# Another order for TensorE in two attention stages: transposes inside the query projection, the second query ahead of the first scores, two output tiles interleaved

## The reference, cut to what matters

```
q = (rmsnorm(q_lat) @ w_uq).reshape(B, S, 8, 128 + 64)      # nope and rope parts
kv = (rmsnorm(kv_lat) @ w_ukv).reshape(B, S, 8, 128 + 128)  # k_nope and v
s = (q_nope k_nope^T + rope(q_rope) rope(k_rope)^T) * scale, causal
y_mla = softmax(s) v * silu(g_mla)
mix = concat([y_mla, y_pool, y_conv]); out = mix @ w_out + b_out
x = layernorm(ALPHA * x + out)
```

```
logits = q k^T * scale + (F[t] - F[s]), causal;  F = cumsum(log_sigmoid(f))
y_b = softmax(logits) v * silu(g_b)
x = x + gate * (concat([y_a, y_b]) @ w_out);  out = rms_norm(x)
```

## Time and profile before

| | us |
|---|---|
| median of 3 runs | 2412.99 (2410.28 to 2414.29) |
| the profiled execution, its time | 2410.3 |
| its span, first to last instruction | 2408.3 |
| TensorE busy | 2355.2 (98%) |
| VectorE busy | 1262.3 (52%) |
| ScalarE busy | 875.1 (36%) |
| GpSimd busy | 411.3 (17%) |
| mean granted clock of TensorE | 0.993 |

### The profile page before, as it was taken

The page is one execution under the profiler, slowest core; times in us unless marked ns, Lnnn a source line. Parts: engine busy times, 40 slices in busy tenths (PEclk is TensorE's granted clock), DMA queues, the critical chain, the costliest instruction groups (busy, mean ns, idle before and its releaser), DMA issues.

```text
span 2408.3 us, 31276 instructions
## 1 busy us (share of the span) xinstructions
PE 2355.2 (98%) x11360; PEld 1954.6 (81%) x11360; DVE 1262.3 (52%) x1970; ACT 875.1 (36%) x1332; POOL 411.3 (17%) x402
## 2 busy tenths in 40 slices
PE   7999999999999999999999999999999999999998
PEld 5888888888887888888788887788878888887887
DVE  8555543476556456543466777643254444444334
ACT  5422223365225422222365223422234444444221
POOL 4111100033113211100042112212002222222000
PEclk9999999999999999999999999999999999999999
DMA  6555553212322555553212323423322222223332
GB/s 245 186 190 177 175 182 113 70 62 70 102 90 71 197 174 174 178 170 131 87 53 71 96 88 112 157 88 105 96 79 88 78 78 78 78 74 133 101 102 79
DMA packets 80906, 281.90 MB, mean 117 GB/s; under 512 B 8896, under 2 KB 13248, under 8 KB 79936
## 3 DMA queue, kind: packets, MB, share of 16 engines
q1 hardware_dynamic: 63968, 217.49, 27.6%
q0 software_dynamic: 16864, 63.45, 7.7%
HBM read 272.51 MB, written 8.39 MB: 117 GB/s over the span
## 4 chain that ended last, share of the span: by engine, by line
PE 81%; issue 8%; DVE 5%; ACT 3%; POOL 1%; DMA 1%; SPq 0%; ACTq 0%; DVEq 0%
PE bank L341 25%; PE bank L343 25%; PE bank L342 25%; DVE w_lo L335 1%; PE bank L2144 1%; ACT w_hi L312 1%; DMA w_raw<-stream 1%; DVE q_rope L1435 0%; DVE bank L1552 0%; DVE x_res L1130 0%; PE bank L2224 0%; PE bank L2225 0%; DVE x_lo L1222 0%; DVE mix_lo L1558 0%; PE bank L2067 0%
## 5 line engine op out<-in xcount | busy, mean ns | idle before, releaser
L343 PE MATMUL bank<-x_hi,w_hi 128*128 128x512 f32 x2896 | 1126.2, 389 | 0.0
L342 PE MATMUL bank<-x_hi,w_lo 128*128 128x512 f32 x2896 | 1125.8, 389 | 0.0
L341 PE MATMUL bank<-x_lo,w_hi 128*128 128x512 f32 (+1 forms) x2384 | 941.8, 395 | 8.3 <-POOL x_lo L418 3.7
L335 DVE SCALAR_TENSOR_TENSOR w_lo<-w_raw,w_hi 128x1024 fp32r<-128x1024 f32 (+1 forms) x384 | 475.5, 1242 | 733.7 <-ACT w_hi L312 732.6
L312 ACT ACTIVATE w_hi<-w_raw 128x1024 fp32r<-128x1024 f32 x390 | 407.7, 1048 | 942.6 <-PE bank L343 903.0
L343 PEld LDWEIGHTS bank<-x_hi,w_hi 128*128 128x128 f32 x2896 | 544.0, 188 | 113.5
L342 PEld LDWEIGHTS bank<-x_hi,w_lo 128*128 128x128 f32 x2896 | 544.9, 188 | 107.1 <-issue 2.2
L341 PEld LDWEIGHTS bank<-x_lo,w_hi 128*128 128x128 f32 x2384 | 448.2, 188 | 101.1 <-issue 6.1
L341 PE MATMUL bank<-mix_lo,w_hi 128*128 128x512 f32 (+1 forms) x656 | 255.3, 389 | 1.1 <-issue 0.9
L425 POOL TENSOR_SCALAR probs<-probs,stats 128x128 f32<-128x128 f32 (+3 forms) x128 | 138.4, 1087 | 643.8 <-DVE stats L1541 643.8
L341 PEld LDWEIGHTS bank<-mix_lo,w_hi 128*128 128x128 f32 x656 | 123.9, 189 | 26.2 <-issue 1.4
(11 more groups left out here) (337 smaller groups left out, 2158.7 us busy)
## 6 DMA issues: line engine op xcount, KB each, us to landing
w_raw<-stream SPq DMA_DIRECT2D x390, 512.0 KB, 3.5
ada_w<-wada POOLq DMA_DIRECT2D x96, 512.0 KB, 4.8
x_tokens<-xN SPq DMA_DIRECT2D x4, 1024.0 KB, 8.7
x_res<-xT SPq DMA_DIRECT2D x16, 256.0 KB, 10.6
x_res_spill<-x_res POOLq DMA_DIRECT2D x8, 512.0 KB, 6.1
x_res<-x_res_spill POOLq DMA_DIRECT2D x8, 512.0 KB, 7.5
outT<-x_res SPq DMA_DIRECT2D x16, 256.0 KB, 2.2
cond_b<-cond POOLq DMA_DIRECT2D x2, 1024.0 KB, 6.1
```

What stands on the lines that cost most here:

```text
L335: nc.vector.scalar_tensor_tensor(out=WL[:, slot, :cols[n]], in0=RAW[:, slot, :cols[n]], scalar=1.0, in1=WH[:, slot, :cols[n]].bitcast(F32) ...
L341: nc.tensor.matmul(out, wh, xl, start=first, stop=False)
L342: nc.tensor.matmul(out, wl, xh, start=False, stop=False)
L343: return nc.tensor.matmul(out, wh, xh, start=False, stop=last)
```

## The change

It alters only the order of instructions: TensorE's in three places, and one ScalarE instruction.

- Heads 2 to 7: `trans1` of blocks 0 and 1 moves from ahead of the query projection to the middle of it, behind its second step.
- Heads 0 and 1: `q_proj(1)` moves ahead of the scores of head 0. In head 1 the value projection comes ahead of block 2's transposes and of the rope projection.
- The first two output tiles of a layer are issued as one list of 32 steps: steps 0 to 14 of the first, 0 to 9 of the second, step 15 of the first, 10 to 15 of the second. The transposes of head 7 come one block at a time behind steps 1, 3, 6 and 9, `pv1` behind steps 7 and 12.
- Second block, first pair: its scores lie at steps 7, 10, 13 and 15.
- Second block, last pair: the work at steps 7, 9, 11, 13 goes to 10, 12, 15, 17, and ScalarE does the last gate right behind the last exponential.

```diff
@@ scalar
             softmax_exp(last, 3, BANKS_2)
+            gate(PAIRS - 1)
             for i in range(QB):
                 for k in MIX_BEHIND[i]:
                     mix2(k)
                 pt_hi(last, i)
-                if i == 1:
-                    gate(PAIRS - 1)
@@ tensor, project(out, u, cols, k0, kt, mid={})
                                         XH[:, k0 + k, :], XL[:, k0 + k, :], k == 0, k == kt - 1)
+                        for work in mid.get(k, ()):
+                            work()
@@ tensor, layer
+                def tr(h, *blocks):
+                    return lambda: [trans1(h, i) for i in blocks]
                 for h in range(HEADS):
                     k_proj(h)
-                    if h:
-                        trans1(h - 1, 0)
-                        trans1(h - 1, 1)
-                    q_proj(h)
-                    if h:
-                        trans1(h - 1, 2)
-                    if h % 2 and h < HEADS - 1:
-                        rope_proj(h // 2 + 1)
-                    v_proj(h)
+                    if h == 0:
+                        q_proj(0)
+                        v_proj(0)
+                        q_proj(1)
+                    elif h == 1:
+                        tr(0, 0, 1)()
+                        v_proj(1)
+                        tr(0, 2)()
+                        rope_proj(1)
+                    else:
+                        q_proj(h, {1: [tr(h - 1, 0, 1)]})
+                        tr(h - 1, 2)()
+                        if h % 2 and h < HEADS - 1:
+                            rope_proj(h // 2 + 1)
+                        v_proj(h)
...
-                tile(l, T_OUT, 0, (S["mix_lo"], KT * l), MIX_ORDER, source=mix,
-                     mid={0: [tr(0), tr(1)], 3: [tr(2)], 4: [pr(0)], 6: [tr(3)], 9: [pr(1)]})
-                tile(l, T_OUT + 1, 1, order=MIX_ORDER, source=mix)
+                def out_pair(mid):
+                    steps = [(0, n) for n in range(KT - 1)] + [(1, n) for n in range(10)]
+                    steps += [(0, KT - 1)] + [(1, n) for n in range(10, KT)]
+                    for at_step, (t, n) in enumerate(steps):
...
+                        pe.wait_ge(S["mix_lo"], KT * l + n + 1)
...
+                out_pair({1: [tr(last_head, 0)], 3: [tr(last_head, 1)], 6: [tr(last_head, 2)], 7: [pr(0)],
+                          9: [tr(last_head, 3)], 12: [pr(1)]})
@@ tensor, second_half
-                return {0: [do(scores2, p, 1, 3)], 2: [do(trans2, p, 1, 0)], 4: [do(trans2, p, 1, 1)],
-                        7: [do(pv2, p, 1, 0), do(trans2, p, 1, 2)], 9: [do(pv2, p, 1, 1), do(trans2, p, 1, 3)],
-                        11: [do(pv2, p, 1, 2)], 13: [do(pv2, p, 1, 3)]}
+                at = (0, 2, 4, 10, 12, 15, 17) if isinstance(p, int) and p == PAIRS - 1 else (0, 2, 4, 7, 9, 11, 13)
...
@@ tensor, pair
-                tile(B2, s + 2, 1, mid={4 + 3 * q: [do(scores2, p, 0, q)] for q in range(QB)}, i=i)
+                tile(B2, s + 2, 1, mid={(at, 4 + 3 * q)[not first]: [do(scores2, p, 0, q)]
+                                           for q, at in enumerate((7, 10, 13, 15))}, i=i)
```

More of the change, by code:

```diff
@@ L1986, in layer, with project @@
                 in_tile(IN_TILES - 1)
-                def project(out, u, cols, k0, kt):
+                def project(out, u, cols, k0, kt, mid={}):
                     slot, before, _ = unit(l, POS_HEAD + u)
@@ L2013, in k_proj, with q_proj @@
                     project(PS[1 if h else 2][:, :], PAIR_UNITS * p + 1, 2 * P * b, 12, 2).then_inc(S["k_mm"], 1)
-                def q_proj(h):
+                def q_proj(h, mid={}):
                     p, b = h // 2, h % 2
@@ L2019, in q_proj @@
                         pe.wait_ge(S["in_ev"], EV_TILES * (l + 1))
-                    project(PS[0][:, :], PAIR_UNITS * p + 2 * b, 0 if b else 4 * P, 8, 4).then_inc(S["q_mm"], 1)
+                    project(PS[0][:, :], PAIR_UNITS * p + 2 * b, 0 if b else 4 * P, 8, 4, mid).then_inc(S["q_mm"], 1)
                 def v_proj(h):
@@ L2109, in layer @@
                     scores(h, 3)
-                def tr(i):
-                    return lambda: trans1(HEADS - 1, i)
+                last_head = HEADS - 1
                 def pr(half):
-                    return lambda: pv1(HEADS - 1, half)
+                    return lambda: pv1(last_head, half)
                 def mix(k):
                     return XH[:, k, :], MLO[:, k, :]
-                tile(l, T_OUT, 0, (S["mix_lo"], KT * l), MIX_ORDER, source=mix,
-                     mid={0: [tr(0), tr(1)], 3: [tr(2)], 4: [pr(0)], 6: [tr(3)], 9: [pr(1)]})
-                tile(l, T_OUT + 1, 1, order=MIX_ORDER, source=mix)
+                def out_pair(mid):
+                    steps = [(0, n) for n in range(KT - 1)] + [(1, n) for n in range(10)]
+                    steps += [(0, KT - 1)] + [(1, n) for n in range(10, KT)]
+                    for at_step, (t, n) in enumerate(steps):
+                        k, col0 = MIX_ORDER[n], (n % 8) * P
+                        slot, before, _ = unit(l, 2 * (T_OUT + t) + n // 8)
+                        pe.wait_ge(w_lo, before + 1)
+                        pe.wait_ge(S["mix_lo"], KT * l + n + 1)
+                        xh, xl = mix(k)
+                        last = products(PS[t][:, :], WH[:, slot, col0:col0 + P], WL[:, slot, col0:col0 + P],
+                                        xh, xl, n == 0, n == KT - 1)
+                        if (t, n) in ((0, 7), (0, KT - 1), (1, KT - 1)):
+                            last.then_inc(w_used, 2 if (t, n) == (0, KT - 1) else 1)
+                        for work in mid.get(at_step, ()):
+                            work()
+                out_pair({1: [tr(last_head, 0)], 3: [tr(last_head, 1)], 6: [tr(last_head, 2)], 7: [pr(0)],
+                          9: [tr(last_head, 3)], 12: [pr(1)]})
                 pe.wait_ge(S["out_ev"], KT * l + 1)
@@ L2256, in second_half @@
             def second_half(p):
-                return {0: [do(scores2, p, 1, 3)], 2: [do(trans2, p, 1, 0)], 4: [do(trans2, p, 1, 1)],
-                        7: [do(pv2, p, 1, 0), do(trans2, p, 1, 2)], 9: [do(pv2, p, 1, 1), do(trans2, p, 1, 3)],
-                        11: [do(pv2, p, 1, 2)], 13: [do(pv2, p, 1, 3)]}
+                at = (0, 2, 4, 10, 12, 15, 17) if isinstance(p, int) and p == PAIRS - 1 else (0, 2, 4, 7, 9, 11, 13)
+                works = ([do(scores2, p, 1, 3)], [do(trans2, p, 1, 0)], [do(trans2, p, 1, 1)],
+                         [do(pv2, p, 1, 0), do(trans2, p, 1, 2)], [do(pv2, p, 1, 1), do(trans2, p, 1, 3)],
+                         [do(pv2, p, 1, 2)], [do(pv2, p, 1, 3)])
+                return dict(zip(at, works))
             def pair(p, first):
```

## The result

| | kernel before | changed kernel |
|---|---|---|
| median of 13 runs each, taken side by side | 2410.35 us (2407.17 to 2414.29) | 2417.22 us (2414.33 to 2418.82) |
| profiled execution | 2410.3 us, span 2408.3 | 2418.11 us, span 2416.2 |

The ratio is 1.0024, 95% interval 1.0017 to 1.0032: slower by 4 to 8 us. The forecast was 2418.0 us. With more runs the median of before fell from 2412.99 to 2410.35 us, so the forecast time is nearly met from a base 2.6 us too high: I forecast 5 us more, and the medians are 6.9 us apart (by the ratio, 5.8). The two profiled spans are 7.85 us apart.

A forecast was written before the change was run, and what follows sets the result against it. TensorE, busy 98% of the span, was taken as the bound, leaving only its waits and clock to win. The terms +4.0 + 2.9 - 0.7 - 3.7 + 3.4 gave +5.9 us; 5.0 was added to the median: 2418.0 us, range 2411 to 2423.

The forecast's parts named there:

- Heads 0 and 1: New order of the first two heads in both layers: 2.3 us slower in layer 0, 1.7 in layer 1, +4.0 us together.
- in head 1 the value projection goes ahead of the rope projection: Head 1, both layers: this delays the rope projection's end by 1.45 us, plus a new 0.75 us wait for `pt_lo`.
- It waits just as long: Head 1's query projection, moved ahead of head 0's scores, still waits 1.90 us for `qn_lo`, whose bank it writes; nothing won.
- Heads 2 to 7: Blocks 0 and 1 transposed 1.4 us later, inside the query projection: costed at nothing, at worst 3.6 us over two layers.
- Output tiles: Interleaved tiles: 2.05 us of waits go, `mix_lo` waits of 0.9 (step 6) and 2.6 us (step 12) come; +1.45 us a layer.
- Second block: First pair -0.7 us, its wait moving to `v_t`; last pair -3.7 us, of which 2.7 is half clock; 2.6 us wait stays.
- The clock in the new gaps: Three new 2.6 us gaps, step 12 in two layers and the last pair's step 8: two falls of the clock, +3.4 us.
- The base: Median of the kernel before, taken as 2.7 us above its profiled execution of 2410.3 us; 5.0 us, not 5.9, added to it.
- head 1's order is hidden: Rival: head 2's wait comes from GpSimd alone, not the rope projection's end, so 4.0 us go; 2414.0 us, chance 0.12.
- the copies come in time: Rival: ScalarE's copies behind the transposes are not what steps 6, 12 and `v_t` wait for; 2407.4 us, faster, chance 0.08.
- The clock staying up in the new gaps: Rival: no fall of TensorE's clock in the three new gaps, 3.4 us less; 2414.6 us, chance 0.22.
- its worst case of 2.7 us in each: Rival: the clock falls for long in all three new gaps, 3 x 2.7 instead of 3.4 us; 2422.7 us, chance 0.18.

## Why the prediction was right, and where it was not

**The waits** came where and for what they were forecast, within 0.1 us: `qn_lo` 1.85 (1.9), `pt_lo` 0.73 (0.75), `mix_lo` 0.90 (0.9) and 2.57 (2.6), `v_t` 1.56 (1.6), the gate 2.49 (2.6). Step 8 was computed for 2.0 us behind the start of the table load; it came 1.99 us behind it (2225.51 and 2227.50), and the gate's activation 1.30 us behind it. So the drain that the page "ScalarE: Activation LUTs" of the Trainium skill puts on top of the load ("What ACT_TABLE_LOAD costs") is not seen at this place, in either trace. In both, the load itself started within 0.1 us of the end of ScalarE's work before it.

**Heads 0 and 1**: right in size, incomplete in cause. Forecast +2.3 and +1.7 us; from the wait for `qn_lo` to head 2's first scores it measured +2.28 (27.83 to 30.11 us) and +3.04 (27.07 to 30.11), of which in layer 1 a fall of the clock is a part. In nine kernels, 18 layers, the old order takes 99.8 to 100.1 us without a fall and 100.6 to 101.5, in the mean 101.1, with one; the new order took 102.9 to 103.05, with a fall, four times out of four. Like against like that is +1.8 us a layer, 3.6 in all, and the whole kernel without this part is 3.8 us faster (2.7 by the ratios). The step "in head 1 the value projection goes ahead of the rope projection" was given the whole cost, and the query projection's move none ("It waits just as long"). The run without the value projection's move still costs 1.0 us in layer 0 and 1.4 in layer 1, like against like: the query projection was the cover of the bank's turn, and taking it away is more than half of the 1.8 us.

**Heads 2 to 7**: costed at nothing. The stretches with and without that part are 0.2 us a layer apart at most (100.11 against 99.9, no fall), less than its bound of 3.6 and less than a run can tell.

**Output tiles**: +1.45 a layer forecast, +1.7 measured in four layers without a fall. A term mis-sized by a quarter of a microsecond; its mechanism, ScalarE held by block 3's transposes, carried 1.86 of the 2.6 us of step 12's wait. The rest is set by the six copies and by `pv1`, as the early transposes showed; I had called nothing there a second bound.

**Second block**: first pair -0.68 (-0.7 forecast). Last pair -3.5 (-3.7): -0.9 us of waits and -2.6 us of clock. The clock's share is no property of the new order alone: the old order had the fall in the traces of six of the eight kernels that kept it, and not in the other two; of the three with the change's own order it fell in one.

**The clock in the new gaps** is the step that failed, in size. Forecast: two falls among three gaps, +3.4 us. In the changed kernel it fell in one, step 12 of layer 1 (30.93 us for the stretch against 29.36 in layer 0, so 1.6 us). Over all kernels that have such gaps it fell in three of nine. Instead it also fell behind the `qn_lo` wait of layer 1, where before it had not, and that I had taken as unchanged: +3.04 us there against a forecast of 1.7. The two norm stages ran 1.7 us longer (+0.68 and +0.97): in the first the same 3.4 us at half clock came at another place, and the second has 10.2 us at half clock where before has 6.8. I had no term for that. So the sum of +5.9 us on the profiled execution came to +7.8. Of the 1.9 us between, some 1.1 are clock by the stretches (1.8 less in the new gaps, 2.9 more elsewhere) and 0.5 the output tiles' own waits. Together with the -2.7 of the last pair the forecast had +0.7 us of clock, and the mean clocks of all executions, 0.9935 before and 0.9932 after, put it at about 0.5: near in total, but at other places than forecast, which is luck.

**The base.** Adding 2.7 us to the profiled execution because three runs had a median above it was wrong: of 13 runs the median is the profiled execution's own time. The two errors, the base 2.6 us too high and the step to the median 1.9 too low, nearly cancel in 2418.0. That the time was met within 0.8 us is in part luck; the waits were not.

**The rivals.** That head 1's order is hidden is refuted (heads part alone +3.3 us, and 3.8 in the whole). That the copies come in time is refuted by the waits. The clock staying up in the new gaps, and its worst case of 2.7 us in each, are both refuted for this execution: one fell, for 1.6 us.

**What stays open.** The medians of the four parts alone add up to +1.8 us (by their ratios +0.5), and the whole measures +6.9 (+5.8). Each part is known to 2.2 us, so the sum to 4.4, and the gap is about as large as that. The waits are the same alone and together, and the granted clocks on record account for most of the gap. The second block's part has a mean clock of 0.9949 against 0.9935 before. Over all executions of the 14 kernels 0.001 of clock goes with 1.6 us. At an equal clock the parts' mean times are then +3.6, 0.0, +3.4 and -2.2 us, in all +4.8, and the whole's +6.0. This is an estimate, and it also takes out what an order itself does to the clock; no run fixed the clock, and why it falls in one execution and not in the next stays open.

## What to carry to other kernels

Work put ahead of a wait fills it only if it doesn't need the same event, and the event may be hidden in a bank that it writes: the query projection waited for `qn_lo` just as the scores did, the key projection did not. Before an instruction is taken out of an order, look at what it stood between: here it was the cover of a bank's turn between a writer and the next, and without it the next one waited 1.6 us. An interleaving should begin with the steps whose input exists, and whatever its producer needs from the same engine should come first; moving both made a loss of 1.7 us a layer into a gain of 2.25.

## What the runs showed of the hardware that was not expected

TensorE's clock answers to gaps of 2 to 3 us, but not each time. Behind equal gaps of 2.5 to 2.6 us it fell to 1.2 GHz in three of nine cases, each time for 3.4 us, which cost about 1.6 us. Behind the 1.9 us for `qn_lo` it fell in 8 of 18 layers in the old order and in 5 of 6 when the query projection stood there, though the gap is the same. With one trace for each kernel that is no rate of either order. And the clock of a stage that no edit touches differs from trace to trace: the layer norm behind layer 1 ran at half clock for 3.4, 6.8 or 10.2 us in kernels with the same instructions there. That the edits ahead of it did this is not shown, since executions of one kernel differ too: those of the kernel before have mean clocks of 0.991 to 0.995 and times 8 us apart. Here are 50 us around it, before and changed (stretch, length, busy time of TensorE, weight loads, VectorE, ScalarE, GpSimd, then granted clock, DMA share, GB/s):

```profile
1470.00:1520.00 50.00, 48.42 (x218) 38.27 (x217) 42.73 (x74) 28.94 (x42) 17.39 (x14) 0.93 0.25 87
```

```profile
1480.00:1530.00 50.00, 49.11 (x214) 38.98 (x213) 40.74 (x71) 26.93 (x40) 16.93 (x14) 0.90 0.24 84
```

So single profiles of two kernels can differ by 1 to 3 us with no difference in their waits, which is as much as half of what was to be explained here.
